# Two phases per chunk in the feed-forward stages, and other PSUM banks for the first output pair

## The reference, cut to what matters

```python
def _swiglu(x, w_in, w_out):                       # ffn 0, 1 (first block)
    gate, up = jnp.split(x @ w_in, 2, axis=-1)
    return (jax.nn.silu(gate) * up) @ w_out

def swiglu(h, wg, wu, wd):                         # ffn 2 to 5 (second block)
    return (jax.nn.silu(h @ wg) * (h @ wu)) @ wd
...
h = h + 0.5 * _swiglu(_rmsnorm(h, ffn1_norm[i]), ffn1_w_in[i], ffn1_w_out[i])
...
for i in range(DEPTH_2):
    mod = c_act @ ada_w[i] + ada_b[i]              # 1024 x 9216 a layer
    sh1, sc1, g1, sh2, sc2, g2, sh3, sc3, g3 = jnp.split(mod, N_MOD, axis=-1)
    h = modulate(rms_norm(x, ln_ffn1[i]), sh1, sc1)
    x = x + 0.5 * g1[:, None, :] * swiglu(h, ffn1_wg[i], ffn1_wu[i], ffn1_wd[i])
```

## Time and profile before

| what | value |
|---|---|
| runs, median (lowest to highest) | 1617.88 us (1616.21 to 1619.92), 3 runs |
| profiled execution | 1616.3 us |
| its span, first to last instruction | 1614.5 us |
| TensorE clock granted, mean | 0.975 |
| PE busy | 1525.9 us (95%) |
| DVE busy | 1195.4 us (74%) |
| ACT busy | 884.1 us (55%) |
| POOL busy | 13.0 us (1%) |
| DMA | 341.72 MB, mean 212 GB/s |

### The profile page before, as it was taken

How to read it: one execution, slowest core, us unless ns; L and a number is a source line. 1 busy time by engine, 2 the same in 40 slices (tenths; PEclk the granted TensorE clock), 3 DMA queues, 4 the chain that set the end, 5 groups by cost and what they waited for, 6 DMA issues and landing times.

```text
span 1614.5 us, 22916 instructions
## 1 busy us (share of the span) xinstructions
PE 1525.9 (95%) x9384; PEld 1349.8 (84%) x9384; DVE 1195.4 (74%) x1506; ACT 884.1 (55%) x1317; POOL 13.0 (1%) x33
## 2 busy tenths in 40 slices
PE   7997999899998999998999999989999999999998
PEld 6886889798877898877888888778888888988887
DVE  5778779968887777777767698878776656676664
ACT  6554554465555475555467684555645544575542
POOL 2000000000000000000000000000000000000000
PEclk9999999799998999999999999999999999999999
DMA  8877845149778756778744267878565574555552
GB/s 290 287 261 251 293 161 183 53 140 322 262 236 296 247 187 210 261 252 273 255 131 150 86 229 253 282 265 274 174 205 183 171 224 158 164 171 182 177 189 79
DMA packets 295560, 341.72 MB, mean 212 GB/s; under 512 B 6035, under 2 KB 256043, under 8 KB 295456
## 3 DMA queue, kind: packets, MB, share of 16 engines
q1 hardware_dynamic: 293488, 334.72, 63.2%
q0 software_dynamic: 1968, 5.54, 1.0%
HBM read 339.17 MB, written 2.63 MB: 212 GB/s over the span
## 4 chain that ended last, share of the span: by engine, by line
PE 57%; DVE 18%; ACT 13%; issue 7%; DMA 5%; SPq 0%; ACTq 0%; DVEq 0%
PE banks L1655 26%; PE banks L1656 13%; ACT w_hi L513 8%; DVE w_lo L981 7%; PE banks L1587 4%; PE banks L1589 4%; PE banks L1588 4%; DMA ada<-in_ada_w 3%; DMA raw<-in_ffn_w_in 2%; DVE arena L1298 2%; DVE silu_g L1062 1%; DVE gu L1070 1%; DVE gu L1067 1%; ACT banks L656 1%; DVE xn L1045 1%
## 5 line engine op out<-in xcount | busy, mean ns | idle before, releaser
L981 DVE TENSOR_TENSOR w_lo<-raw,w_hi 128x2048 fp32r<-128x2048 f32 (+1 forms) x250 | 559.3, 2239 | 296.6 <-ACT w_hi L513 295.8
L1655 PE MATMUL banks<-xs,w_hi 128*128 128x512 f32 x1952 | 696.6, 400 | 3.7 <-DVE w_lo L981 3.7
L513 ACT ACTIVATE w_hi<-raw 128x2048 fp32r<-128x2048 f32 (+1 forms) x250 | 465.4, 1865 | 182.6 <-PE banks L1656 144.9
L1656 PE MATMUL banks<-xs,w_lo 128*128 128x256 f32 x1952 | 551.4, 282 | 0.0
L1655 PEld LDWEIGHTS banks<-xs,w_hi 128*128 128x128 f32 x1952 | 371.4, 190 | 93.2 <-DVE w_lo L981 5.0
L1655 PE MATMUL banks<-g_pair,w_hi 128*128 128x512 f32 x1056 | 377.8, 400 | 27.6 <-ACT banks L656 21.5
L1656 PEld LDWEIGHTS banks<-xs,w_lo 128*128 128x128 f32 x1952 | 372.4, 191 | 0.0
L1656 PE MATMUL banks<-g_pair,w_lo 128*128 128x256 f32 x1056 | 299.7, 284 | 0.0
L1655 PEld LDWEIGHTS banks<-g_pair,w_hi 128*128 128x128 f32 x1056 | 202.8, 192 | 73.5 <-ACT banks L656 22.5
L1656 PEld LDWEIGHTS banks<-g_pair,w_lo 128*128 128x128 f32 x1056 | 202.9, 192 | 0.0
L1089 DVE SCALAR_TENSOR_TENSOR ada_acc<-ada,c_act,ada_acc 128x512 f32<-128x512 f32 x252 | 187.6, 748 | 13.8 <-DMA ada<-in_ada_w 9.0
(11 more groups left out here) (297 smaller groups left out, 1765.1 us busy)
## 6 DMA issues: line engine op xcount, KB each, us to landing
ada<-in_ada_w SPq DMA_DIRECT2D x72, 1024.0 KB, 6.8
raw<-in_ffn_wg SPq DMA_DIRECT2D x44, 1024.0 KB, 5.3
raw<-in_ffn_wu SPq DMA_DIRECT2D x44, 1024.0 KB, 5.4
raw<-in_ffn_w_in SPq DMA_DIRECT2D x43, 1024.0 KB, 5.5
raw<-in_ffn_wd SPq DMA_DIRECT2D x32, 1024.0 KB, 5.3
raw<-in_ffn_w_out SPq DMA_DIRECT2D x16, 1024.0 KB, 5.3
raw<-in_ffn_wd SPq DMA_DIRECT2D x16, 768.0 KB, 4.5
raw<-in_attn_w_qkv SPq DMA_DIRECT2D x12, 1024.0 KB, 5.2
```

The lines of the kernel that those rows point to most:

```text
L513: act.activation(w_hi[:, s, 0:width(c)], raw[:, s, 0:width(c)], ACT.Copy).then_inc(hi_ready, 1)
L981: dve.tensor_tensor(w_lo[:, s, 0:width(c)], raw[:, s, 0:width(c)], w_hi[:, s, 0:width(c)].bitcast(F32), ALU.subtract).then_inc(lo_ready, 1)
L1655: pe.matmul(o, wh[:, k, m], pair, start=first, stop=False, skip_group_check=True)
L1656: return pe.matmul(o[:, 0:T], wl[:, k, m], pair[:, 0, :], start=False, stop=last, skip_group_check=True)
```

## The change

Nothing is added to or taken from what is computed. Five things are moved.

1. In the gated chunks ACT does the bank copy first, then w_hi, then the silu or the high part of the product; DVE does the bank sum (and the multiplication) first, then w_lo, then the modulation steps. In the down chunks DVE does `two_sided` and `early` ahead of w_lo.
2. The first two output pairs change banks: the first now uses 6-7, the second 0-1. Turns at chunks 22 to 24 use bank 1, those before them too.
3. The wait ahead of chunk 22 is now for the product of step 9, which frees banks 6-7. The wait for the stores is ahead of chunk 25 (the second pair) instead, and ahead of 31 as before.
4. ACT's product that begins a modulation block moves one chunk later, to the chunk of its first DVE step.
5. In the last chunk DVE does `early` and `fold` ahead of w_lo of chunk 35.

```diff
-        GATE_UP_AT, DOWN_AT = (4, 6, 2), (0, 6, 4, 2)
+        GATE_UP_AT, DOWN_AT = (4, 6, 2), (6, 0, 4, 2)
...
-            return banks8[:, 1 if at < GATED else 2 if at < FFN_CHUNKS - len(ROWS) else 6, :]
+            return banks8[:, 1 if at < GATED + len(ROWS) else 2 if at < FFN_CHUNKS - len(ROWS) else 6, :]
...
-                        if ADA_FROM[b] - 1 == a:
+                        if ADA_FROM[b] == a:
                             ada_product(b)
...
                 for a in range(2, GATED + 1):          # ScalarE
+                    if a % 2:
+                        gate_low(a // 2)
+                    elif a > 2 or not d:
+                        up_low(a // 2 - 1)
                     split(c0 + a + 2)
-                    if a % 2 == 0:
-                        if a > 2 or not d:
-                            up_low(a // 2 - 1)
+                    if a % 2:
+                        silu_of_sum(a // 2)
+                    else:
                         gu_high(a // 2 - 1)
-                    else:
-                        gate_low(a // 2)
-                        silu_of_sum(a // 2)
                     ada_work(a)
...
                 for a in range(2, FFN_CHUNKS):         # VectorE
-                    if a == FFN_CHUNKS - 1 and f < 4:
-                        modulation(f // 2, f % 2)
-                    split(c0 + a + 2)
-                    if a <= GATED and a % 2 == 0:
+                    steps = ADA_STEPS.get(a, 0)
+                    if a == FFN_CHUNKS - 1:
+                        if f < 4:
+                            modulation(f // 2, f % 2)
+                        early(2)
+                        fold(xn, sq_added, 3 * PAIRED_NO[nxt], sq_folded, 2 * AFTER_NO[nxt])
+                        if plain:
+                            fold(ub, plain_added, 0, ev("plain_folded"), 0)
+                        split(c0 + a + 2)
+                    elif a <= GATED and a % 2 == 0:
                         if a > 2 or not d:
                             gu_mul(a // 2 - 1)
-                        ada_part(a)
+                        split(c0 + a + 2)
+                        ada_part(steps)
                         gu_low(a // 2 - 1)
                     elif a <= GATED:
                         gate_sum(a // 2)
-                        ada_part(a)
+                        split(c0 + a + 2)
+                        ada_part(steps)
                     else:
                         pair, part = divmod(a - GATED, 3)
                         if part == 0:
                             two_sided((2 * pair - 2, 2 * pair - 1))
                         if part == 2 and pair:
                             early(pair - 1)
-                        ada_part(a)
+                        split(c0 + a + 2)
+                        ada_part(steps)
...
                     if at >= FFN_CHUNKS - len(ROWS):   # TensorE, in turn()
-                        pe.wait_ge(x_ready, 8 * n + 4)
-                    elif at >= GATED:
+                        pe.wait_ge(x_ready, 8 * n + 2)
+                    elif at >= GATED + len(ROWS):
                         pe.wait_ge(silu_done, s0 + STEPS)
...
-                if f < 4:
-                    pe.wait_ge(ada_stored, ADA_FFN * f + sum(at + 2 < GATED for at in ADA_TO))
+                pe.wait_ge(gu_ready, s0 + STEPS - 1)
                 for a in range(GATED, FFN_CHUNKS):
                     pair, part = divmod(a - GATED, 3)
                     turned(a)
-                    if pair == 3 and part == 0 and f < 4:
-                        pe.wait_ge(ada_stored, ADA_FFN * f + sum(at + 2 < FFN_CHUNKS - len(ROWS) for at in ADA_TO))
+                    if pair in (1, 3) and part == 0 and f < 4:
+                        pe.wait_ge(ada_stored, ADA_FFN * f + sum(at + 2 < a for at in ADA_TO))
```

More of the change, by code:

```diff
@@ L1076, in ffn, with ada_part @@
                 ada_at = [ADA_FFN * f * ADA_PER]
-                def ada_part(a):
-                    for _ in range(ADA_STEPS.get(a, 0) if f < 4 else 0):
+                def ada_part(count):
+                    for _ in range(count if f < 4 else 0):
                         done, k = ada_at[0] // ADA_PER, ada_at[0] % ADA_PER + 1
@@ L1188, in ffn @@
                         low(p_lo[:, :, :], ub[:, 0:2, :], p_hi[:, :, :]).then_inc(ev("p_lo"), 1)
-                fold(xn, sq_added, 3 * PAIRED_NO[nxt], sq_folded, 2 * AFTER_NO[nxt])
-                if plain:
-                    fold(ub, plain_added, 0, ev("plain_folded"), 0)
                 for k in (6, 7):
```

## The result

| | before | changed |
|---|---|---|
| median of the runs | 1617.27 us (1616.21 to 1619.92, 4 runs) | 1542.09 us (1541.33 to 1542.63, 4 runs) |
| span of the profiled execution | 1614.5 us | 1540.8 us |
| granted clock, mean | 0.975 | 0.990 |
| ratio of the runs | | 0.9532, 95% interval 0.9516 to 0.9549 |

The changed kernel is 75.2 us faster. The forecast was 1545 us in a range of 1538 to 1562; its sum had the profiled execution at 1542.8, and that took 1542.63 us.

What follows compares the result with a forecast made beforehand. PE, busy 95%, waits where ACT and DVE fall behind passing work back and forth: at the modulation's transposes and ahead of chunk 22. 31.8 + 27.6 + 9.8 + 4.3 = 73.5 us off 1616.3 gives 1542.8; forecast 1545, range 1538 to 1562.

Steps and rivals of the forecast that it cites:

- gated chunks, ffn 0 to 3: New order in the gated chunks: the transposes' waits go and windows shrink to 115.5 to 122.3 us, 31.8 us won.
- gaps ahead of chunk 22: PE's four waits for ACT's stores at the first down matmul of ffn 0 to 3 all go, 27.6 us.
- down chunks: Down windows of ffn 0 to 3 fall to 62.9 us without the lower clock behind the gap, 9.8 us won.
- stage ends: Ends of ffn 0, 1, 2 and 4 come down to 3.5 us, ffn 3's end gives 1.5; together 4.3 us.
- Backlog passed between ScalarE and VectorE: Gated chunks: a pair is 12.2 us of work passed back and forth where PE wants 11.3; backlog paid at chunk 22.
- Banks and the new wait: Ahead of chunk 22: step 9's product is ready 8 us before, so all four gaps go, 27.6 us.
- The product moved one chunk later: ACT's product starting a modulation block: nothing won; 16 us lost if DVE's cover in the down chunks were gone.
- VectorE full but not the bound: Gated chunks: DVE needs 9.9 to 10.6 us a pair of PE's 11.3.
- the sign that I had named, nearly 95%: Sign of being right: DVE busy nearly 95% of the gated windows, no longer waiting most for w_hi there.
- The clock: ffn 0 to 3: slow stretches go with the gaps; granted clock 1.00 through the gated and down windows.
- the rival of stretches in new places: Slow stretches stay, in other places, behind short waits; keeping them all gives 1561 us; chance 0.08.
- The rival's limit of 285 GB/s: DMA becomes the bound: at 285 GB/s each of four stages takes 186 us instead of 178, 1576 us; chance 0.04.

Runs made afterwards that it cites:

- experiment 3: Changed kernel with ScalarE's old order (w_hi ahead of the bank copy) put back in the gated chunks, VectorE's order left new: 1542.16 us, ratio 0.9543.
- experiment 4: Changed kernel with VectorE's old order (w_lo ahead of the sums) put back in the gated chunks, ScalarE's order left new: 1644.59 us, ratio 1.0177.
- 10: Kernel before with only VectorE's order in the gated chunks changed (sums and product ahead of w_lo): 1582.67 to 1587.95 us, one outlier left out, ratio 0.9806.
- 11: Kernel before with two edits, VectorE's new order in the gated chunks and ScalarE's product one chunk later: 1550.79 us, ratio 0.9590.
- experiment 1: Changed kernel with the first pair's old banks and the old wait for the stores ahead of chunk 22 put back: 1541.43 us, ratio 0.9537.
- experiment 2: Kernel before with only the new banks and the new waits at chunks 22, 25 and 31: 1604.47 us, ratio 0.9926.
- experiment 6: Changed kernel with ScalarE's product that begins a modulation block one chunk earlier again: 1558.43 us, ratio 0.9647.
- experiment 7: Changed kernel with the product one chunk earlier only for the three blocks that begin in the down chunks: 1540.63 us, ratio 0.9529.

## Why the prediction was right, point by point

**The sum by its terms.** From the windows before and after:

| term | predicted | measured |
|---|---|---|
| gated chunks, ffn 0 to 3 | 8.3 + 7.5 + 9.5 + 6.5 = 31.8 | 8.77 + 7.44 + 9.70 + 5.85 = 31.8 |
| gaps ahead of chunk 22 | 27.6 | 27.6 |
| down chunks | 9.8 | 2.54 + 2.52 + 2.47 + 2.09 = 9.6 |
| stage ends | 4.3 | 4.6 |
| sum | 73.5 | 73.6, of 73.7 of the span |

That this fits so well has one main reason: the target was measured in the same trace. Ffn 4 showed TensorE's pace without waits, and everything in the sum but the stage ends is a distance to it. The last tenths are luck: ffn 0 and 2 won 0.5 and 0.2 us more than forecast and ffn 3 0.65 less, which is the growth of its wait for w_lo, a term that I had taken as fixed.

**Backlog passed between ScalarE and VectorE.** Right, and shown from both sides: experiments 3, 4, 10 and 11. Two things I had not seen. VectorE's half of the order does all of it once the product is moved too; I priced both halves together. And the loop is not made longer than TensorE's 11.3 us by the modulation alone: in ffn 4 of the kernel before it already takes 11.51 us a pair (the rows in experiment 4), which the work done ahead at the stage's start covers. With so little to spare, every piece that the modulation puts into ScalarE's queue makes TensorE wait. The even chunk of 6.8 us that I read in the earlier trace rows has the product in it (477.76 - 477.05 = 0.7 us); the sum and the multiplication behind w_lo account for the other 6.1.

**Banks and the new wait.** The forecast that all four gaps go was right; putting them under the heading of the banks was not. The gap is won by the order (experiment 1). The banks alone win 11 us (experiment 2), and beside the full new order nothing that can be measured; they cover tenths of a us where only VectorE's half of it is there (experiment 11).

**The product moved one chunk later.** I took nothing for it, with a price of 16 us if VectorE's cover in the down chunks were gone. Nothing was lost by the move, as said. But I weighed it only as a risk and missed that it was a condition: leaving it where it was would have cost 16.3 us (experiment 6), through the blocks of the gated chunks and not those of the down chunks (experiment 7). That this is near my 16 us is chance: mine was for another edit and another cause. ScalarE now gets to the product sooner after the load is issued, and the load takes longer. For the block that begins at chunk 19 of ffn 1, the kernel before issued the load at 469.91; it landed 7.1 us later, and the product began at 477.05 without a wait, since ScalarE was late itself. In experiment 6 the load was issued at 447.04, ScalarE was free for the product at 450.57, 3.5 us later, and the load landed 9.2 us after its issue, at 456.2. So of the 5.65 us of waiting some 3.6 come from ScalarE being sooner and 2.1 from the slower load. My expectation there repeated the mistake, by counting TensorE's lead and not what stood behind the product in ScalarE's queue.

**VectorE full but not the bound.** Right in kind: 0.55 us a chunk more still fits. Its busy time is as forecast, 102.87 us for ffn 1's ten pairs and 103.27 for ffn 3's, 10.3 us a pair. That is 84 to 89% of the four gated windows; the sign that I had named, nearly 95%, was above my own sum and did not show. In ffn 1's gated window VectorE's waits for w_hi fell from 21.0 to 8.7 us, but they are still its longest in sum.

**The clock.** All slow stretches in ffn 0 to 3 but the one at ffn 0's start are gone, and none came up elsewhere in the feed-forward stages. By the Trainium skill, "TensorE: Matmul & The Clock Gate", Part 1 (the HAM clock gate), the clock falls after idle time; the trace agrees, with windows at 1.00 where 0.96 stood, and the rival of stretches in new places did not come. Of the short waits my weighing of the clock had shown one place only. In the kernel before, the wait of 2.57 us at 459.21 has no slow stretch behind it, but one of 2.56 us ahead of the transposes at 1043.44 has:

```profile
1045.20:1047.40 2.20, 2.20 (x8) 1.91 (x8) 2.17 (x3) 0.00 (x0) 0.00 (x0) 0.50 1.06 380
```

So the gated chunks' gain holds some slow work too, behind waits of 1.81, 3.57 and 2.56 us in ffn 0, 2 and 3.

**Stage ends.** The first scaling comes 3.40 us after the last matmul began at the ends of ffn 0 and 1, and 3.52 at those of ffn 2 and 4, against 4.1 to 4.4 before (4.30 for ffn 4 in the earlier trace rows); the rest, 1.5 us, is ffn 3's end.

**DMA.** 310 GB/s over a whole gated window, at a share of 0.91, and TensorE loses nothing to it inside the windows of ffn 1. The rival's limit of 285 GB/s is not there. In ffn 1's gated chunks the median landing went from 5.4 to 6.1 us for a weight chunk and from 6.5 to 7.3 for a modulation load; in ffn 3 it stayed, 7.4 and then 7.2 for the latter.

## What to carry to other kernels

Where two engines hand work to each other in order, put what the other waits for first and the bulk work, which nobody waits for yet, behind it; and try each engine's half by itself, since here, with the other edits in place, VectorE's half alone won as much as both, and with ScalarE's alone the kernel was 1.8% slower than before. A gap at a barrier may be backlog from far before it: look at the stage's pace against a stage without the side work before changing the barrier. And when an engine gets faster, recount every load that its neighbours wait for at the head of their queues: the product that waited 3.7 us for its loads in all waited 65.5 us once the chunks came faster and it stood where it had.

## What was not expected of the hardware

ScalarE's copies out of PSUM took 0.60 us in the changed kernel and 0.57 before (L624: 596 ns against 574, L634: 598 against 575). They now run at the very start of TensorE's next chunk. With ScalarE's old order (experiment 3), where they run behind w_hi again, their median is back at 577 ns, against 600 in the changed kernel; and with the copies first but ScalarE late (experiment 4) it is 578 to 580. So it goes with the time at which they run and not with their place in the queue; what they meet there is not shown. And DMA took 13% more data per us in ffn 1's gated window (310 against 275 GB/s) with landings 12 to 13% longer; two points don't tell how it goes on from there.
